# Second block's attention in a two-block layer kernel: value columns held in TensorE and divided, turned probabilities streamed, two heads on the two column halves

## What is computed

```python
# 512 tokens, query token q, key token k, head h (64 columns each)
logits[h, q, k] = (q_h . k_h) / 8, with keys outside the selected set at -inf
p[h, q, k]      = exp(logits - max_k) / sum_k exp(logits - max_k)
hC[q, 64h:64h+64] = sum_k p[h, q, k] * v[k, 64h:64h+64]
out = concat([hA, hB, hC], axis=-1) @ w_out          # hA mLSTM, hB LRU, hC attention
```

## Time and profile before

| | before |
|---|---|
| median of 3 runs | 1533.55 us (1533.29 to 1533.76) |
| time of the profiled execution | 1534.0 us |
| span of the profiled execution | 1532.1 us |
| PE busy | 1520.7 us, 99% of the span |
| DVE busy | 1101.7 us, 72% |
| ACT busy | 646.7 us, 42% |
| stretch of the second attention | about 1058 to 1114 us of the span |

### The profile page before, as it was taken

The page is one execution under the profiler, slowest core; times in us unless marked ns, Lnnn a source line. Parts: engine busy times, 40 slices in busy tenths (PEclk is TensorE's granted clock), DMA queues, the critical chain, the costliest instruction groups (busy, mean ns, idle before and its releaser), DMA issues.

```text
span 1532.1 us, 25451 instructions
## 1 busy us (share of the span) xinstructions
PE 1520.7 (99%) x9994; PEld 1362.9 (89%) x9994; DVE 1101.7 (72%) x1550; ACT 646.7 (42%) x1015; POOL 55.4 (4%) x115
## 2 busy tenths in 40 slices
PE   9999999999999999999999999999999999999998
PEld 8999999999999999999988888878888888888887
DVE  5889888888655587777764458988748887887123
ACT  5224545555643434434334335744645333333122
POOL 0000111111000000000000020000000000000000
PEclk9999999999999999999999999999999999999999
DMA  6333222232233243232232443231132333332221
GB/s 180 83 93 100 56 72 68 57 83 56 56 102 92 83 110 82 82 109 82 66 94 81 115 109 83 57 83 42 56 110 56 110 101 91 89 103 96 110 83 55
DMA packets 235360, 131.64 MB, mean 86 GB/s; under 512 B 20985, under 2 KB 228741, under 8 KB 235285
## 3 DMA queue, kind: packets, MB, share of 16 engines
q1 hardware_dynamic: 234900, 130.40, 30.3%
q0 software_dynamic: 384, 0.20, 0.0%
HBM read 128.48 MB, written 2.10 MB: 85 GB/s over the span
## 4 chain that ended last, share of the span: by engine, by line
PE 91%; DVE 5%; ACT 2%; issue 0%; DMA 0%; SPq 0%; DVEq 0%; ACTq 0%
PE psP L726 32%; PE psS L726 25%; PE psP L791 8%; PE psS L1432 4%; PE psP L1432 4%; PE psP L748 4%; PE psP L1122 3%; PE psP L1300 1%; DVE conv L2170 1%; PE psS L1300 1%; PE psP L969 1%; DVE wl L2050 1%; PE psP L879 1%; PE psS L928 1%; PE psS L1189 1%; PE psP L956 1%
## 5 line engine op out<-in xcount | busy, mean ns | idle before, releaser
L2050 DVE TENSOR_TENSOR wl<-raw,wh 128x2048 fp32r<-128x2048 f32 x124 | 284.1, 2291 | 174.8 <-ACT wh L1487 173.4
L1487 ACT ACTIVATE wh<-raw 128x2048 fp32r<-128x2048 f32 x124 | 237.0, 1911 | 207.1 <-PE psS L1432 74.3
L726 PE MATMUL psP<-xh,wh 128*128 128x264 f32 (+3 forms) x1184 | 296.0, 312 | 1.2 <-DVE wl L2050 0.5
L726 PE MATMUL psP<-xl,wh 128*128 128x264 f32 (+3 forms) x1184 | 291.4, 309 | 0.0
L726 PE MATMUL psP<-xh,wl 128*128 128x264 f32 (+3 forms) x1184 | 290.3, 308 | 0.0
L726 PE MATMUL psS<-xh,wh 128*128 128x256 f32 (+2 forms) x880 | 210.3, 305 | 0.4 <-DVE hT L2079 0.4
L726 PE MATMUL psS<-xl,wh 128*128 128x256 f32 (+2 forms) x880 | 208.1, 303 | 0.0
L726 PE MATMUL psS<-xh,wl 128*128 128x256 f32 (+2 forms) x880 | 207.2, 302 | 0.0
L726 PEld LDWEIGHTS psP<-xh,wh 128*128 128x128 f32 x1184 | 192.2, 189 | 16.3 <-issue 2.2
L726 PEld LDWEIGHTS psP<-xl,wh 128*128 128x128 f32 x1184 | 192.7, 189 | 12.0 <-issue 0.2
L726 PEld LDWEIGHTS psP<-xh,wl 128*128 128x128 f32 x1184 | 192.2, 189 | 11.9
(11 more groups left out here) (483 smaller groups left out, 2429.7 us busy)
## 6 DMA issues: line engine op xcount, KB each, us to landing
raw<-in_w_in_dram SPq DMA_DIRECT2D x74, 512.0 KB, 4.9
raw<-in_w_up_dram SPq DMA_DIRECT2D x44, 512.0 KB, 4.6
raw<-in_ffn_up_dram SPq DMA_DIRECT2D x44, 512.0 KB, 4.9
raw<-in_ffn_down_dram SPq DMA_DIRECT2D x22, 512.0 KB, 3.9
raw<-in_w_out_dram SPq DMA_DIRECT2D x16, 512.0 KB, 4.7
raw<-in_w_down_dram SPq DMA_DIRECT2D x16, 384.0 KB, 3.6
raw<-in_w_down_dram SPq DMA_DIRECT2D x16, 320.0 KB, 4.0
raw<-in_w_conv_out_dram SPq DMA_DIRECT2D x8, 512.0 KB, 4.6
```

Source lines behind the costliest of these rows:

```text
L726: ins = mm(dst, W[:, s, half, k, 0:rows], Y[:, k, c0 + o:c0 + o + w], start=(k == 0 and p == 0), stop=(k == KT - 1 and p == 2))
L1487: fn(wh[:, n % 2], raw[:, n % 2], ACT.Copy).then_inc(s_hi, 1)
L2050: V.tensor_tensor(wl[:, n % 2], raw[:, n % 2], wh[:, n % 2].bitcast(f32), ALU.subtract).then_inc(s_lo, 1)
```

## The change

Per query block, the probabilities are now divided by their sums on ACT before they are turned (`divide_probs`, four instructions, one per head, each with a semaphore step; `turn` waits for the heads that it needs). `weighted` is now one call per block, after the last load of the block. It holds 64 value columns of a head in the array and streams the 128 turned probabilities; even heads write to PSUM partitions 0 to 63, odd heads to 64 to 127. So the output comes with features on partitions: `attention_back` and `osb` are gone, and `attention_hi(i)` / `attention_lo(i)` make `ch`/`cl[:, 6:8]` per block from `psP[1][:, 1]`. `invert_sums` moves ahead on DVE. The diff, cut to its core:

```diff
@@ PE
-                pe.wait_ge(s_pe, i + 1)
+                pe.wait_ge(s_pw, AT_H * i + h1)
...
-            def weighted(i, load, h0, h1):
+            def weighted(i, load):
...
-                if h0 == 0:
-                    if i:
-                        pe.wait_ge(s_pd, i)
-                    else:
-                        pe.wait_ge(s_ea, evacuated(2 * (n + 11) + 1)[1])
-                for h in range(h0, h1):
-                    o = 256 * (i % 2) + 64 * h
+                if i:
+                    pe.wait_ge(s_hcl, i)
+                else:
+                    pe.wait_ge(s_ea, evacuated(2 * (n + 11) + 1)[1])
+                for f in range(2):
+                    o = 256 * (i % 2) + 128 * f
                     for j in range(t + 1):
-                        ins = mm(psP[1][:, 1, o:o + 64], PT[:, h, 128 * j:128 * (j + 1)], av[:, j, 64 * h:64 * (h + 1)],
-                                 start=(j == 0), stop=(j == t))
-                if h1 == AT_H:
-                    ins.then_inc(s_po, 1)
-
-            def attention_back(i):
-                t = BLOCKS[i]
-                pe.wait_ge(s_pd, i + 1)
-                if i == 0:
-                    pe.wait_ge(s_lk, TT)
-                for f in range(2):
-                    ins = tr(scores_ps[:, f, 128 * t:128 * (t + 1)], osb[:, t, 128 * f:128 * (f + 1)], ident[:])
-                ins.then_inc(s_pb, 1)
+                        for b in range(2):
+                            h = 2 * f + b
+                            ins = mm(psP[1][64 * b:64 * b + 64, 1, o:o + 128], av[:, j, 64 * h:64 * (h + 1)],
+                                     PT[:, h, 128 * j:128 * (j + 1)], start=(j == 0), stop=(j == t))
+                ins.then_inc(s_po, 1)
...
-                        pe.wait_ge(s_hcl, k - 5)
+                        pe.wait_ge(s_hcl, TT)
...
             turn(2, 9, 3, 4)
-            weighted(2, 8, 2, 3)
             out_tokens(0, 0, (2, 3))
-            weighted(2, 9, 3, 4)
+            weighted(2, 9)
             turn(3, 10, 0, 4)
-            for i in range(2):
-                attention_back(i)
             out_tokens(1, 0, (0, 1))
             out_tokens(1, 0, (2, 3))
-            weighted(3, 10, 0, 4)
-            attention_back(2)
-            for k in range(2, 4):
+            weighted(3, 10)
+            for k in range(2, KT):
                 out_tokens(k, 0, range(TT))
-            attention_back(3)
-            for k in range(4, KT):
-                out_tokens(k, 0, range(TT))
@@ ACT
-            def scale_outputs(i):
+            def divide_probs(i):
+                t = BLOCKS[i]
+                act.wait_ge(s_pn, i + 1)
+                for h in range(AT_H):
+                    p = prt[t][:, h, :]
+                    fn(p, p, ACT.Copy, scale=att[:, 1, i, h:h + 1]).then_inc(s_pw, 1)
+
+            def attention_hi(i):
                 t = BLOCKS[i]
                 act.wait_ge(s_po, i + 1)
-                act.wait_ge(s_pn, i + 1)
-                for h in range(AT_H):
-                    o = 256 * (i % 2) + 64 * h
-                    ins = fn(osb[:, t, 64 * h:64 * (h + 1)], psP[1][:, 1, o:o + 64], ACT.Copy, scale=att[:, 1, i, h:h + 1])
-                ins.then_inc(s_pd, 1)
+                o = 256 * (i % 2)
+                fn(ch[:, 6:8, 128 * t:128 * (t + 1)], psP[1][:, 1, o:o + 256].rearrange("p (f q) -> p f q", f=2), ACT.Copy).then_inc(s_hc, 1)
...
             values(1)
+            divide_probs(0)
             hi(n + 13)
             copy_probs(0, 0, 0, 2)
             copy_probs(0, 1, 2, 4)
             attention_exps(1)
-            scale_outputs(0)
+            attention_hi(0)
+            divide_probs(1)
...
             attention_exps(2)
-            scale_outputs(1)
+            attention_hi(1)
+            divide_probs(2)
             copy_probs(2, 6, 0, 1)
             hi(N_WO2)
...
             copy_probs(2, 9, 3, 4)
+            divide_probs(3)
             gelu(2)
             lru_hi(1)
+            attention_hi(2)
             copy_probs(3, 10, 0, 4)
             lru_hi(2)
-            scale_outputs(2)
             hi(N_WO2 + 1)
-            scale_outputs(3)
-            act.wait_ge(s_pb, TT)
-            for f in range(2):
-                fn(ch[:, 6 + f, :], scores_ps[:, f, :], ACT.Copy).then_inc(s_hc, 1)
+            attention_hi(3)
@@ DVE
+            def attention_lo(i):
+                t = BLOCKS[i]
+                tok = slice(128 * t, 128 * (t + 1))
+                o = 256 * (i % 2)
+                dve.wait_ge(s_hc, i + 1)
+                V.tensor_tensor(cl[:, 6:8, tok], psP[1][:, 1, o:o + 256].rearrange("p (f q) -> p f q", f=2),
+                                ch[:, 6:8, tok].bitcast(f32), ALU.subtract).then_inc(s_hcl, 1)
```

More of the change, by code:

```diff
@@ L284, in program @@
         prt = [pr0, pr1, pr2, pr3]
-        osb = at("osb", [128, TT, AT_W], start=va_start)
         lg = at("lg", [128, LG, S], start=mo_start)
@@ L412, in program @@
         s_po = sem("attention_outputs")
-        s_pd = sem("attention_outputs_scaled")
-        s_pb = sem("attention_turned_back")
+        s_pw = sem("attention_probs_divided")
         s_hc = sem("attention_hi")
@@ L1364, in _ @@
             turn(0, 1, 2, 4)
-            weighted(0, 0, 0, 2)
             lru_side(0, 2, 4)
-            weighted(0, 1, 2, 4)
+            weighted(0, 1)
             lru_side(0, 4, 8)
@@ L1372, in _ @@
             turn(1, 3, 1, 2)
-            weighted(1, 2, 0, 1)
             lru_side(1, 2, 4)
             turn(1, 4, 2, 3)
-            weighted(1, 3, 1, 2)
             lru_side(1, 4, 6)
             turn(1, 5, 3, 4)
-            weighted(1, 4, 2, 3)
             lru_side(1, 6, 8)
-            weighted(1, 5, 3, 4)
+            weighted(1, 5)
             lru_side(2, 0, 2)
@@ L1387, in _ @@
             turn(2, 7, 1, 2)
-            weighted(2, 6, 0, 1)
             lru_side(2, 6, 8)
             turn(2, 8, 2, 3)
-            weighted(2, 7, 1, 2)
             out_tokens(0, 0, (0, 1))
             turn(2, 9, 3, 4)
-            weighted(2, 8, 2, 3)
             out_tokens(0, 0, (2, 3))
-            weighted(2, 9, 3, 4)
+            weighted(2, 9)
             turn(3, 10, 0, 4)
-            for i in range(2):
-                attention_back(i)
             out_tokens(1, 0, (0, 1))
             out_tokens(1, 0, (2, 3))
-            weighted(3, 10, 0, 4)
-            attention_back(2)
-            for k in range(2, 4):
+            weighted(3, 10)
+            for k in range(2, KT):
                 out_tokens(k, 0, range(TT))
-            attention_back(3)
-            for k in range(4, KT):
-                out_tokens(k, 0, range(TT))
-            pe.wait_ge(s_pd, TT)
+            pe.wait_ge(s_hcl, TT)
             for k in range(4):
@@ L2674, in _ @@
                                        ch[:, g, :].bitcast(f32), ALU.mult, ALU.subtract).then_inc(s_hl, 1)
+            def attention_lo(i):
[5 more added lines that the diff above has]
+                                ch[:, 6:8, tok].bitcast(f32), ALU.subtract).then_inc(s_hcl, 1)
             mask_logits(0)
             select(3, 8, 10)
+            invert_sums(0)
             mask_logits(1)
-            invert_sums(0)
             lo(n + 13)
-            select(3, 10, 13)
+            select(3, 10, 12)
+            invert_sums(1)
+            select(3, 12, 13)
+            attention_lo(0)
             scaled(lg[:, 0, :], 2 * (n + 12))
@@ L2683, in _ @@
             mask_logits(2)
-            invert_sums(1)
             scaled(lg[:, 1, :], 2 * (n + 12) + 1)
+            invert_sums(2)
+            attention_lo(1)
             mask_logits(3)
-            invert_sums(2)
             lo(N_WO2)
@@ L2695, in _ @@
             lru_lo(1)
+            attention_lo(2)
             lru_lo(2)
             lo(N_WO2 + 1)
-            for f in range(2):
-                dve.wait_ge(s_hc, f + 1)
-                V.tensor_tensor(cl[:, 6 + f, :], scores_ps[:, f, :], ch[:, 6 + f, :].bitcast(f32), ALU.subtract).then_inc(s_hcl, 1)
+            attention_lo(3)
             lo(N_WO2 + 2)
```

## The result

| | us | runs |
|---|---|---|
| before, median (range) | 1533.69 (1533.29 to 1534.27) | 22 |
| changed kernel, median (range) | 1536.31 (1534.59 to 1537.15) | 22 |
| ratio | 1.0015, 95% interval 1.0009 to 1.0021 | |
| profiled execution after: span, time | 1534.9, 1536.69 | |

The account below looks back on a forecast made before the run. The DVE and ACT chain was taken to bound the kernel up to the first out_tokens, PE's own work behind it: +2.2 - 0.5 = +1.7 us, median 1535.3 us, 0.1% slower, counted as no change; range 1533.9 to 1538.2.

Parts of the forecast that it names:

- The joint: Start of the first out_tokens on PE, 1098.76 us, released by the chain over DVE and ACT; forecast to move +2.2 us.
- The reciprocals: Ahead of the joint on DVE: invert_sums(0) leaves the stretch, invert_sums(1) stays; they only change places, no time added.
- ACT's part: Exponentials of block 2 to the split: divide_probs(2) adds 2.48 us, scale_outputs(1) replaced by attention_hi(1) gives -0.57 us.
- The four divisions: divide_probs(2) on ACT, ahead of load 6's copy and hi(N_WO2): four at 0.62 us, +2.48 us, bounds 2.1 and 2.8.
- PE ahead of the joint gains nothing: PE's saved work before the first out_tokens becomes waits, some 5 us in all, 1.6 us of it at turn(0, 1).
- Behind the joint: PE's work from the first out_tokens on: 2.1 us pairs + 0.8 form changes - 2.5 old products - 0.88 turns = -0.5 us.
- the changes of form: PE going into and out of the split array, two groups behind the joint: 0.8 us, bounds 0 and 0.8.
- the second rival: Behind the joint: no loss going into and out of the split array, 0.8 us less, 1534.5 us; chance 0.13.
- The first and third rivals: Behind the joint: first, column halves one after other, +3.9 us, chance 0.17; third, also exposed loads, 1539.6 us, chance 0.04.
- The sum: Whole kernel: +2.2 us ahead of the joint and -0.5 us behind it, +1.7 us; 1535.3 us for the median.
- The step that failed: PE's new waits ahead of turn(0, 1), turn(2, 6) or turn(2, 7) and out_tokens: no fall of the granted clock expected.
- The fourth rival: Joint moves and more waits follow it, turn(2, 9) behind its copy, ACT's longer list: up to 1.3 us more; chance 0.10.

Follow-up runs that it names:

- the kernel with the filler: The changed kernel with two needless fp32 products of 512 columns in PE's wait ahead of the first out_tokens (also called the third experiment): 1534.91 us, ratio 1.0009.
- the fourth experiment: The changed kernel with the loops over key blocks and heads exchanged, so neighbouring products of a block use the same column half: 1536.65 us, ratio 1.0020.
- the last experiment: The 1531.12 us kernel (early split, copies ahead of gelu, out_tokens pieces in PE's waits) with load 0's copy put ahead of hi(n + 13) on ACT: 1531.22 us.
- the first experiment: The changed kernel with chunk N_WO2 split earlier, hi before block 2's exponentials on ACT, lo behind scaled(lg[1]) on DVE: 1534.05 us, ratio 1.0004.

## Why the prediction came out as it did

- **The joint.** Forecast +2.2 us, measured 2.14. By its terms: up to the exponentials of block 2 the chain grew by 0.26 us (logits to first exponential: 22.52 us, from 1066.92 to 1089.44; before 22.26, from 1067.22 to 1089.48). `attention_lo(0)` delayed what stands behind it by 0.34 (1078.79 to 1079.13), forecast 0.33. The reciprocals were misread: invert_sums(0) leaves the stretch, but invert_sums(1) doesn't "stay", it comes in, from behind the maxima of block 2 (1089.37 before) to between the rounds of select (1077.21). At 0.08 and 0.09 us the two cancel, which is luck. From the exponentials to the split ACT's part grew by 1.89 us (1089.44 to 1095.57; before 1089.48 to 1093.72), forecast 2.48 - 0.57 = 1.91. The four divisions take 2.47 us from the first start to the next instruction (1092.62 to 1095.09), forecast 2.48. From the split to the joint nothing changed (5.03 and 5.04 us).
  The two ends of ACT's part. Before, in order of time on ACT, the first exponential of block 2:

```profile
1089.48 0.72 ACT L1849 ACTIVATE pr<-pr,att 128x512 f32<-128x512 f32 x1 [2.95 <-DVE att L2582]
```

After, the first exponential, the divisions and the split:

```profile
1089.44 0.72 ACT L1825 ACTIVATE pr<-pr,att 128x512 f32<-128x512 f32 x1 [3.55 <-DVE att L2563]
...
1092.62 2.56 ACT L1839 ACTIVATE pr<-pr,att 128x512 f32<-128x512 f32 x4
...
1095.57 1.90 ACT L1463 ACTIVATE wh<-raw 128x2048 fp32r<-128x2048 f32 x1
```

- **PE ahead of the joint gains nothing.** Right: new waits at turn(0, 1), turn(2, 6) and the joint, 4.4 us, with the small ones 5.1 in all where 5 were forecast. At turn(0, 1) it is 0.96 us and not 1.6. It is shown from both sides: work moved into the waits is gained (1531.12 us), the same moves without waits to fill gain 0.35 at most, and a wait that is taken away comes back at the joint.
- **Behind the joint.** Forecast -0.5 us. In the kernel with the filler the 97th product of out_tokens (the first of the second half) starts 26.17 us after the joint (1126.57 - 1100.40), before 26.77 (1125.53 - 1098.76): -0.6. PE at this product, before and with the filler:

```profile
1125.53 0.40 PE L1300 MATMUL psP<-wh,ch 128*128 128x512 f32 x1
```

```profile
1126.57 0.40 PE L1289 MATMUL psP<-wh,ch 128*128 128x512 f32 x1
```

  Its two changed groups take 1.90 and 0.59 us. By 20 pairs x 0.107 that is 2.1 us of products and some 0.35 of the changes of form in front of the next instruction; with the slower start of the follower (0.10 us at the second group), the changes of form cost 0.5 to 0.7 us, where 0.8 was taken and the second rival had nothing. That is about the 0.1 us by which -0.6 differs from -0.5. The first and third rivals (no pairs, exposed loads) are refuted for the code as it is: a group of 32 records took 1.90 us, not over 3.
- **The sum.** +2.14 - 0.60 = +1.5 us; the lower group of times is at +1.3. Forecast +1.75. Right to within 0.5 us.
- **The step that failed** is the last one, "a fall of the granted clock in these waits is not expected". It falls behind the very wait of 2 us that the prediction had placed correctly, and by the times it does so in 12 of 22 runs, for 1.7 us each. The median of 1536.3 is the forecast's mechanism plus this. The stated bounds held it only through rivals with other causes: that 1536.3 lies in them is luck.
- **The fourth rival**, more waits behind the joint, named the right place: turn(2, 9) with its copy behind the table load. In the changed kernel the late joint covers it, and it came only when the split was made early.

What stays open: why the clock falls in some runs and not in others of the same program; and which waits are a risk. Both falls seen in a trace stand behind waits of 1.95 and 1.99 us, and the fourth experiment's trace has 1.95 us without one. In the last experiment's kernel PE waits 1.39 us and its 11 times lie within 1.0 us of each other, with no second group. But the one run at 1536.22 us of the first experiment's kernel, whose longest wait is 1.44 us, has the time and the mean clock of a fall, so shorter waits can't be called safe. No trace here shows a wait of PE between 1.46 and 1.95 us.

## What to carry to other kernels

A faster form of an engine's work is gained only where that engine sets the end: find the points where another engine's chain meets it, and move work that is ready from behind such a point into the waits in front of it. Here the product form alone lost 2.6 us in the median and gained 2.4 once three small pieces, two copies and a split had been moved. Count a wait of PE as long as those here, about 2 us, as a risk to its clock as well: the price is paid behind the wait, where PE may be what counts, and even needless products in the wait can be the cheaper choice.

## What the runs showed of the hardware

- A wait in which PE did 0.15 us of work in 2.10 was followed by 3.4 us at 1.2 GHz in the profiled execution; by their times 12 of 22 runs of the changed kernel did so, and with the wait filled none of 11.
- Two fp32 products on different column halves of the array run together: 0.109 us for a pair of records with 128 streamed columns each, which start 6 to 7 ns apart, though both use all 128 rows and write one bank. One half alone takes the same 0.109 us for a single record.
- Their weights don't show: "TensorE: Matmul & The Clock Gate" of the Trainium skill (Part 3, The mechanism) lets loads overlap running products only where the row group differs. Here all rows are shared, each record has a load of its own (0.137 us in the kernel of the third experiment, two of them within 7 ns), PE's loads are busy 88% beside 99% of products, and a pair costs no more than its streaming. The rule doesn't hold in this trace, as the prediction had assumed.
- In an order with one half after the other, TensorE still overlapped them, by the starts across several instructions (2.50 us for 32 records, between the 1.90 in pairs and 3.4 one by one).
